# A decoder step on one core: 64 cache copies of 1 MB between the loads, and two samples' keys moved ahead of a weight

## The chip, the cores and the metric

The kernel runs on one core of a Trainium2 chip. The metric is the device time of one execution in microseconds (us). Before the change the median of three runs is 1412.86 us (1412.8 to 1414.62).

## The reference, cut to what matters

One layer is computed for a prompt of 256 tokens and for 8 samples of 4 new tokens each: a mixer with windowed attention, cross-attention to 256 memory tokens, then a mixture of 32 experts. All of it is float32. The parts that the change touches:

```python
k_all = jnp.concatenate([cache_k_win[l], k], axis=1)      # 8 samples, 2048 old rows + 4 new ones, 512 wide
v_all = jnp.concatenate([cache_v_win[l], v], axis=1)
o_a = merge_branches([dilated_branch_sample(q, k_all, v_all, w, d, rel_bias) for (w, d) in DILATED])
...
mk, mv = mem_kv(mem_prompt, g_mem[l], w_xk[l], w_xv[l])   # keys and values of the memory tokens
...
xs = xs + moe(rmsnorm(xs, g_ff[l]), *moe_w)               # 32 experts: w_gate_up 1024x2048, w_down 1024x1024
...
k_win_sample = k_all[:, n_new:]                           # the window moved on by 4 rows: an output
v_win_sample = v_all[:, n_new:]
```

The last two lines make 16 blocks of 2,044 old rows (4.19 MB each, 67 MB in all) that go unchanged from one place in DRAM to another. No engine computes on them: they are plain DMA transfers, here called cache copies. The attention of a sample reads only about 9 rows per partition of its keys and of its values.

## The kernel before, in words

**Work.** The program is written out by hand, engine by engine. It first projects all 288 tokens with `w_in` (TensorE, lines 1436 and 1440), turns and pools, projects the second half of the prompt (line 1520), and then walks over the samples, b = 1 to 7. For each sample VectorE multiplies the window's keys with the four queries (`row`, lines 1129 to 1132, four times a sample), ScalarE takes exponentials, TensorE multiplies with the values (`values`, lines 1628 and 1630). Beside the samples lie `FILL` products: `mk` and `mv`, the memory's keys and values (line 1608), which need `w_xk` and `w_xv`. Then follow the output projection, cross-attention, the router, and a loop over 32 experts (lines 1895 and 1924). The experts' weights go through two buffers, `wide` (gate and up, 8 MB) and `slim` (down, 4 MB), each of which holds one expert; a piece is loaded again as soon as TensorE has read it.

**Buffers of the samples.** `kwin[0]`, `kwin[1]` (the keys of even and odd samples) and `vwin` (values) lie in `wide`, over `w_in`. So a window can be loaded only when the projection has read the pieces of `w_in` below it (`w_read` counts the pieces). A window is four transfers, 1.8 MB together (lines 499 and 502). ScalarE then moves the last rows of a window into place (`late_keys`, `late_values`, line 764) before VectorE or TensorE may use it.

**The order of transfers.** All of this goes out on SyncE's one queue, and the transfers of that queue are served in the order of issue. SyncE waits in its program for what a transfer needs (a free buffer) and then issues it; what stands behind waits too. `copy(n)` issues n cache copies. The list `COPIES` says how many at each of 14 places, and after the first expert's weights `copy(len(pieces))` issues what is left. `slim_round` loads a weight into `slim` (line 495), `window` a sample's keys or values, `step0` the first expert (lines 598 and 602), `step` the others (607 and 610). Before the change a copy is 2 MB, and there are 32 of them: 7 at the first place, 3 between the first expert's two weights, 3 left after them.

Of the kernel before, what the change touches and what calls it, by code (L numbers as in the profile page):

```python
# [8 lines left out]
P = 128  # L9
D = 1024  # L10
KC = D // P
SEQ, DEC_B, DEC_T = 256, 8, 4
# [5 lines left out]
AW = HEADS * HD  # L18
# [80 lines left out]
def build(nc, i, o):  # L99
# [5 lines left out]
    with ctx:  # L105
# [34 lines left out]
        slimf = slim[:, :, :].rearrange("p k n -> p (k n)")  # L140
        kwin = [wf[:, 4608 * s:4608 * s + 4608].rearrange("p (s n) -> p s n", n=AW) for s in range(2)]
        kfirst = slimf[:, 3584:8192].rearrange("p (s n) -> p s n", n=AW)
# [109 lines left out]
        def add(*name):  # L252
            jobs.append(name)
# [14 lines left out]
        for t in range(DEC_T):  # L268
            add("qb", 0, t)
        add("trq", 1), add("trk", 1)  # L270


        COPIES = [7, 1, 1, 1, 1, 2, 1, 2, 2, 2, 3, 2, 1, 3]
        ROUND_AT = {3: 1, 7: 2}
# [11 lines left out]

        add("qb", 1, 0), add("qb", 1, 1)
        for lot in range(2):
# [156 lines left out]
        pieces = []  # L445
        for b in range(DEC_B):
            for src, dst in (("cache_k_win", "k_win_sample"), ("cache_v_win", "v_win_sample")):
                for h in range(2):
                    pieces.append(tuple(ap.rearrange("s h d -> (s h d)").rearrange("(c j a n) -> c a j n", c=2, a=16, j=8)[h]
                                        for ap in (o[dst][0, b, 0:KEEP], i[src][0, b, DEC_T:PAST])))  # L450
# [14 lines left out]
        def _(sp):  # L465
# [4 lines left out]
            load(sp, "gcol", gcol[:, :, :], i["g_all"])  # L470
            load(sp, "rel", rb[0:BUCKETS, :], i["rel_bias"])
            for k in range(KC):
                sp.dma_start(wide[:, k, :], w_in[k]).then_inc(wide_in[k], 16)
            load(sp, "cbias", cb[:, 0:TOEP + 6 * P + 4 * NS], i["c_bias"])
            load(sp, "cfresh", fmask[:, :], i["c_fresh"])
# [4 lines left out]
            load(sp, "iota", iota[:, :], i["c_iota"])  # L480

            def copy(n):
                for _ in range(n):
                    dst, src = pieces.pop(0)
                    sp.dma_start(dst, src).then_inc(stored["copies"], 16)

# [16 lines left out]

            sp.wait_ge(cleared, 1)
            window(kfirst, i["cache_k_win"], 0, k_in[0])
            b, use = place(("tr1", 2, 1))
            sp.wait_ge(bank_full[b], use + 1)
# [8 lines left out]
            copy(COPIES.pop(0))  # L516

            sp.wait_ge(w_read, 5)
            window(kwin[1], i["cache_k_win"], 1, k_in[1])
            sp.wait_ge(w_read, 7)  # L520
# [5 lines left out]
            for b in range(1, DEC_B):  # L526
                if b + 1 < DEC_B:
                    sp.wait_ge(scored, b)
                    window(kwin[(b + 1) % 2], i["cache_k_win"], b + 1, k_in[(b + 1) % 2])
                if b in ROUND_AT:  # L530
                    slim_round(ROUND_AT[b])
                else:
                    copy(COPIES.pop(0))

                bb, use = place(("pv", b - 1))
                sp.wait_ge(bank_full[bb], use + 1)
                window(vwin, i["cache_v_win"], b, v_in)
# [56 lines left out]
            def step0():  # L594

                sp.wait_ge(wide_used, 8)
                for c in range(4):
                    sp.dma_start(wide[:, 2 * c:2 * c + 2, :], gate_up(0, c)).then_inc(wide_in[2 * c], 16)
                copy(COPIES.pop(0))
                for h in range(2):  # L600
                    sp.wait_ge(slim_used, 4 * h + 4)
                    sp.dma_start(slim[:, 4 * h:4 * h + 4, :], down(0, h)).then_inc(slim_in[4 * h], 16)
# [24 lines left out]
            sp.wait_ge(stored["y"], 48)  # L627
            sp.wait_ge(stored["copies"], 16 * 4 * DEC_B)

# [96 lines left out]
        def _(act):  # L726
# [72 lines left out]
            for t in range(2):  # L799
                root(3 + t, P, hn[:, t, :], mkTf[:, 0:D] if t == 0 else mkTf[:, D:2 * D])  # L800
            rows_out(1)
            turned_in(1)
# [42 lines left out]
            unit_exp(0)  # L845
            late_keys(1)
            for lot in range(2):
# [136 lines left out]
        def _(dve):  # L984
# [173 lines left out]
            for b in range(1, DEC_B):  # L1158
                dve.wait_ge(expd, 2 * b)
                share(b - 1, b, P * (UNITS[b - 1][1] + 1))  # L1160
                dve.wait_ge(k_in[b % 2], 64 * (b // 2 + 1))
                dve.wait_ge(late_k, b + 1)
                for t in range(DEC_T):
                    row(b, t)
                    if t < 3:
                        (shift, sums, shares)[t](b - 1)
                    if b >= 2 and t == 0:
                        keep(b - 2)
                    if t == 2:
                        logits(b)  # L1170
                largest_score(b)
# [240 lines left out]
        def _(pe):  # L1412
# [105 lines left out]
            for k in range(KC):  # L1518
# [6 lines left out]
                for t in ROWS_AT.get(k, ()):  # L1525
                    pe.wait_ge(qparts_in, 1)
                    row(0, t)
            turn_rows(1)

# [110 lines left out]

            row(1, 0), row(1, 1)
            for lot in range(2):
# [336 lines left out]
```

## Time and profile before

| what | value |
|---|---|
| median of three runs | 1412.86 us |
| the profiled execution's own time | 1413.55 us |
| its span | 1411.8 us |
| TensorE busy | 1259.9 us (89%) |
| VectorE busy | 482.0 us (34%) |
| ScalarE busy | 234.3 us (17%) |
| DMA, mean over the span | 395 GB/s, 557.14 MB |
| chain that ended last | DMA 50%, PE 38%, DVE 8% |

The span is the stretch between the first and the last instruction of the profiled execution; the execution's own time is 1.75 us more. A busy share is an average over stages that have different limits, so it says little by itself. The rows that are needed stand further down. DMA rows give the time from issue to landing, which contains the time that a transfer waits in the queue.

### The profile page before, as it was taken

To read this page: it belongs to the slowest core of one execution; us is meant where nothing else is said; L and a number is where in the kernel's file an instruction comes from. 1 tells how busy PE (TensorE), PEld (TensorE's weight loads), DVE (VectorE), ACT (ScalarE), POOL (GpSimd) and SP (SyncE) were. 2 spreads that over 40 slices of the span, in tenths; PEclk is the share of its full clock that TensorE was granted. 3 is DMA by queue.
4 is the path that set the end of the run, shared out by engine and by line. 5 is a ranking of instruction groups with operands and counts; after the bars stand their busy time and mean duration, and the time that the engine had idled before them with its cause. 6 is when DMAs were issued, how large, how long until landed. Compare 5 with 4: busy or idle time off the path is not lost.

```text
span 1411.8 us, 16539 instructions
## 1 busy us (share of the span) xinstructions
PE 1259.9 (89%) x6415; PEld 528.3 (37%) x6415; DVE 482.0 (34%) x1019; ACT 234.3 (17%) x460; POOL 68.1 (5%) x69
## 2 busy tenths in 40 slices
PE   6997988988897899999999999999999999999996
PEld 4453333356644433333333333333333333333332
DVE  2267988432326412312132121321213212132124
ACT  1234443211411110110110100111011010011102
POOL 2010000005007000000000000000000000000000
PEclk9998988899997999999999999999999999999998
DMA  9989898998999999999999999999999999999993
GB/s 356 342 307 391 342 394 320 366 385 303 344 365 370 346 417 427 427 428 427 428 429 428 428 430 428 427 430 429 428 428 429 428 428 429 428 428 430 428 427 158
DMA packets 51740, 557.14 MB, mean 395 GB/s; under 512 B 7021, under 2 KB 9301, under 8 KB 15885
## 3 DMA queue, kind: packets, MB, share of 16 engines
q1 hardware_dynamic: 50629, 553.04, 96.0%
q0 software_dynamic: 1072, 3.57, 0.6%
q8 instruction: 26, 0.43, 0.1%
q14 instruction: 13, 0.11, 0.0%
HBM read 552.02 MB, written 71.72 MB: 442 GB/s over the span
## 4 chain that ended last, share of the span: by engine, by line
DMA 50%; PE 38%; DVE 8%; issue 1%; ACT 1%; SPq 1%; DVEq 0%; ACTq 0%
DMA wide<-in_w_gate_up 49%; PE bank L1895 12%; PE bank L1587 3%; PE bank L1608 2%; PE bank L1924 2%; PE bank L1690 2%; PE bank L1630 2%; PE bank L1440 2%; DMA wide<-in_cache_k_win 1%; PE bank L1520 1%; DVE small L1132 1%; PE bank L1436 1%; PE bank L1678 1%; DVE wide L1129 1%; PE bank L1877 1%
## 5 line engine op out<-in xcount | busy, mean ns | idle before, releaser
L1895 PE MATMUL bank<-wide,att 128*64 128x512 f32 x2048 | 463.3, 596 | 58.6 <-DMA wide<-in_w_gate_up 58.4
L1895 PEld LDWEIGHTS bank<-wide,att 128*64 128x64 f32 x2048 | 139.3, 136 | 362.6 <-issue 228.6
L1924 PE MATMUL bank<-slim,att 128*64 128x512 f32 x1024 | 226.8, 595 | 0.0
L1372 DVE TENSOR_SCALAR att<-bank 128x512 f32<-128x512 f32 x32 | 22.1, 692 | 469.1 <-PE bank L1895 469.1
L1924 PEld LDWEIGHTS bank<-slim,att 128*64 128x64 f32 x1024 | 70.6, 137 | 152.2 <-issue 149.2
L1351 DVE TENSOR_TENSOR x<-x,bank 128x512 f32<-128x512 f32 x68 | 46.6, 686 | 233.0 <-PE bank L1877 226.4
L954 ACT ACTIVATE att<-att 128x512 f32<-128x512 f32 x32 | 20.2, 630 | 517.4 <-DVE att L1372 517.4
L1877 PE MATMUL bank<-tb,att 128*128 128x512 f32 (+1 forms) x192 | 84.7, 611 | 1.8 <-issue 1.3
L963 ACT ACTIVATE tb<-bank 64x512 f32<-64x512 f32 x64 | 37.9, 592 | 234.1 <-PE bank L1924 233.7
L1608 PE MATMUL bank<-slim,ta 128*128 128x512 f32 x128 | 59.7, 621 | 3.0 <-DVE wide L1130 3.0
L1132 DVE TENSOR_REDUCE small<-wide 128x24 f32<-128x1536 f32 x28 | 49.1, 1753 | 1.0
L1844 PE MATMUL bank<-att,mkT 128*128 128x128 bf16 x408 | 46.7, 224 | 1.4 <-DVE att L1302 1.4
L1844 PE MATMUL bank<-att,ta 128*128 128x128 bf16 x408 | 46.3, 224 | 0.0
L1630 PE MATMUL bank<-wide,pr 128*32 128x512 f32 x192 | 34.1, 865 | 10.2 <-DVE pr L1111 10.2
L764 ACT ACTIVATE wide<-wide 32x512 f32<-32x512 f32 x60 | 37.6, 626 | 8.9 <-DMA wide<-in_cache_v_win 5.7
L1608 PEld LDWEIGHTS bank<-slim,ta 128*128 128x128 f32 x128 | 24.7, 198 | 36.8 <-issue 36.8
L1129 DVE TENSOR_TENSOR wide<-wide,bank 128x1024 f32<-128x1024 f32 x28 | 33.9, 1212 | 3.1 <-ACT wide L764 3.0
L1690 PE MATMUL bank<-ta,slim 128*128 128x288 f32 x128 | 33.0, 422 | 2.2 <-DVE ta L1020 2.2
L1844 PEld LDWEIGHTS bank<-att,mkT 128*128 128x128 bf16 x408 | 28.7, 100 | 15.2 <-issue 14.6
L1379 DVE TENSOR_TENSOR att<-att 128x512 f32<-128x512 f32 x32 | 33.4, 1045 | 1.1
L959 ACT ACTIVATE att<-bank 128x512 f32<-128x512 f32 x32 | 19.1, 597 | 74.8 <-PE bank L1915 74.8
L1915 PE MATMUL bank<-ident,att 128*128 128x128 f32 x128 | 21.0, 286 | 11.5 <-DVE att L1379 9.6
(279 smaller groups left out, 1153.4 us busy)
## 6 DMA issues: line engine op xcount, KB each, us to landing
wide<-in_w_gate_up SPq DMA_DIRECT2D x128, 2048.0 KB, 25.5
slim<-in_w_down SPq DMA_DIRECT2D x64, 2048.0 KB, 22.0
out_k_win_sample<-in_cache_k_win SPq DMA_DIRECT2D x16, 2044.0 KB, 19.4
out_v_win_sample<-in_cache_v_win SPq DMA_DIRECT2D x16, 2044.0 KB, 27.8
wide<-in_w_in SPq DMA_DIRECT2D x8, 1024.0 KB, 14.2
wide<-in_cache_v_win SPq DMA_DIRECT2D x8, 1024.0 KB, 4.9
wide<-in_cache_mem_k SPq DMA_DIRECT2D x8, 1024.0 KB, 23.5
wide<-in_cache_mem_v SPq DMA_DIRECT2D x8, 1024.0 KB, 13.0
```

The lines of the kernel that those rows point to most:

```text
L963: ins = A(ye[i // 2][CAP * (i % 2):CAP * (i % 2) + CAP, 512 * h:512 * h + 512], bank_y[CAP * h:CAP * h + CAP, :], ACT.Copy)
L1129: V.tensor_tensor(pd[:, 0:2, :], pair, ps[:, :].unsqueeze(1).broadcast_to([P, 2, AW]), ALU.mult)
L1132: link(V.tensor_reduce(S_[b % 2][:, :, t, :], pd.rearrange("p k (h d) -> p k h d", d=HD), AX.X, ALU.add))
L1351: ins = V.tensor_tensor(dst, dst, bk[:, :], ALU.add)
L1587: ins = M(tk[h][0][0:n, :], left[:, k, t0:t0 + n], slim[:, k, 512 * h:512 * h + 512], start=k == 0, stop=k == KC - 1)
L1608: ins = M(ps[:, :], ta[:, k, P * t:P * t + P], slim[:, k, 512 * h:512 * h + 512], start=k == 0, stop=k == KC - 1)
L1630: ins = M(ps[g, :], flat[:, kind, :], vwin[:, 8 if kind == 2 else 4 * kind + t, :], start=k == 0, stop=False)
L1690: ins = M(ps[:, 0:T], slim[:, k, P * c:P * c + P], ta[:, k, :], start=k == 0, stop=k == KC - 1)
L1844: M(bk[:, c:c + 2 * CAP], hparts[t][:, s, P * k:P * k + P], onehot[:, t, :], start=t == 0 and s == 0, stop=False)
L1877: ins = M(out, back[buf][:, t0:t0 + m], ye[buf][:, 512 * h:512 * h + 512], start=True, stop=True)
L1895: ins = M(bk[half[h], :], rows[:, k, :], wide[:, k, c:c + 512], start=False, stop=k == KC - 1)
L1924: ins = M(bank_y[half[h], :], aT[:, f % 4, f // 4, :], slim[:, f, 512 * h:512 * h + 512], start=f == 0, stop=f == KC - 1)
```

## The change

Cache copies are cut in four pieces a block, where there were two: 64 transfers of 1 MB. Their places change. Six go between the eight pieces of `w_in`, two around the keys of sample 0, one ahead of the keys of sample 2, four between the four pieces of the first expert's gate and up weights; `COPIES` (now counted in MB) is set anew, and nine are left behind the first expert. The two key buffers swap places, so that the keys of sample 1 need three pieces of `w_in` read, where they needed five, and those of sample 2 five; both are now issued ahead of `w_xk`. On TensorE the first two query rows of sample 1 come ahead of turning the second half of the prompt; ScalarE moves that sample's late keys earlier; VectorE does its first row ahead of scaling the first unit's shares.

```diff
-        kwin = [wf[:, 4608 * s:4608 * s + 4608].rearrange("p (s n) -> p s n", n=AW) for s in range(2)]
+        kwin = [wf[:, 4608 * s:4608 * s + 4608].rearrange("p (s n) -> p s n", n=AW) for s in (1, 0)]
...
-        add("trq", 1), add("trk", 1)
+        add("qb", 1, 0), add("qb", 1, 1), add("trq", 1), add("trk", 1)
...
-        COPIES = [7, 1, 1, 1, 1, 2, 1, 2, 2, 2, 3, 2, 1, 3]
+        COPIES = [5, 3, 4, 3, 2, 2, 3, 2, 4, 4, 5, 3, 2, 4]
...
-                for h in range(2):
-                    pieces.append(tuple(ap.rearrange("s h d -> (s h d)").rearrange("(c j a n) -> c a j n", c=2, a=16, j=8)[h]
+                for h in range(4):
+                    pieces.append(tuple(ap.rearrange("s h d -> (s h d)").rearrange("(c j a n) -> c a j n", c=4, a=16, j=4)[h]
...
             for k in range(KC):
                 sp.dma_start(wide[:, k, :], w_in[k]).then_inc(wide_in[k], 16)
+                if 0 < k < KC - 1:
+                    copy(1)
...
             sp.wait_ge(cleared, 1)
+            copy(1)
             window(kfirst, i["cache_k_win"], 0, k_in[0])
+            copy(1)
...
+            sp.wait_ge(w_read, 3)
+            window(kwin[1], i["cache_k_win"], 1, k_in[1])
             sp.wait_ge(w_read, 5)
-            window(kwin[1], i["cache_k_win"], 1, k_in[1])
+            copy(1)
+            window(kwin[0], i["cache_k_win"], 2, k_in[0])
             sp.wait_ge(w_read, 7)
             window(vwin, i["cache_v_win"], 0, v_in)
...
             for b in range(1, DEC_B):
-                if b + 1 < DEC_B:
+                if 1 < b < DEC_B - 1:
                     sp.wait_ge(scored, b)
                     window(kwin[(b + 1) % 2], i["cache_k_win"], b + 1, k_in[(b + 1) % 2])
...
                 for c in range(4):
                     sp.dma_start(wide[:, 2 * c:2 * c + 2, :], gate_up(0, c)).then_inc(wide_in[2 * c], 16)
-                copy(COPIES.pop(0))
+                    copy(1)
+                copy(COPIES.pop(0) - 4)
...
             for t in range(2):
                 root(3 + t, P, hn[:, t, :], mkTf[:, 0:D] if t == 0 else mkTf[:, D:2 * D])
+            late_keys(1)
             rows_out(1)
...
             unit_exp(0)
-            late_keys(1)
...
             for b in range(1, DEC_B):
-                dve.wait_ge(expd, 2 * b)
-                share(b - 1, b, P * (UNITS[b - 1][1] + 1))
+                if b > 1:
+                    dve.wait_ge(expd, 2 * b)
+                    share(b - 1, b, P * (UNITS[b - 1][1] + 1))
...
                     row(b, t)
+                    if b == 1 and t == 0:
+                        dve.wait_ge(expd, 2)
+                        share(0, 1, P)
...
+            row(1, 0), row(1, 1)
             turn_rows(1)
...
-            row(1, 0), row(1, 1)
             for lot in range(2):
```

SyncE's queue around `w_xk` (the weight of the memory's keys), before. `in_cache_k_win` into `wide` is a window of keys, `in_cache_v_win` one of values, and a row whose output begins with `out_` is a cache copy:

```order
L499 DMA wide<-in_cache_k_win 128x2048
L502 DMA wide<-in_cache_k_win 32x2048 x3
L499 DMA wide<-in_cache_v_win 128x2048
L502 DMA wide<-in_cache_v_win 32x2048 x3
L495 DMA slim<-in_w_xk 128x1024 x8
L485 DMA out_k_win_sample<-in_cache_k_win 16x8x4088
L499 DMA wide<-in_cache_k_win 128x2048
L502 DMA wide<-in_cache_k_win 32x2048 x3
L485 DMA out_k_win_sample<-in_cache_k_win 16x8x4088
L499 DMA wide<-in_cache_v_win 128x2048
L502 DMA wide<-in_cache_v_win 32x2048 x3
```

The same place after the change:

```order
L501 DMA wide<-in_cache_k_win 128x2048
L504 DMA wide<-in_cache_k_win 32x2048 x3
L475 DMA out_k_win_sample<-in_cache_k_win 16x4x4088
L501 DMA wide<-in_cache_k_win 128x2048
L504 DMA wide<-in_cache_k_win 32x2048 x3
L501 DMA wide<-in_cache_v_win 128x2048
L504 DMA wide<-in_cache_v_win 32x2048 x3
L497 DMA slim<-in_w_xk 128x1024 x8
L475 DMA out_k_win_sample<-in_cache_k_win 16x4x4088 x3
L475 DMA out_v_win_sample<-in_cache_v_win 16x4x4088 x4
L501 DMA wide<-in_cache_v_win 128x2048
L504 DMA wide<-in_cache_v_win 32x2048 x3
```

The keys of sample 2 moved from behind `w_xk` and a copy to ahead of it. Between `w_xk` and the values of sample 1 there stood 4 MB of copies and the keys of sample 2; now there stand 7 MB of copies.

SyncE's queue around the first expert, before (`w_gate_up` and `w_down` are its weights):

```order
L598 DMA wide<-in_w_gate_up 128x4096 x4
L485 DMA out_v_win_sample<-in_cache_v_win 16x8x4088 x2
L485 DMA out_k_win_sample<-in_cache_k_win 16x8x4088
L602 DMA slim<-in_w_down 128x4096 x2
L485 DMA out_k_win_sample<-in_cache_k_win 16x8x4088
L485 DMA out_v_win_sample<-in_cache_v_win 16x8x4088 x2
```

And after the change:

```order
L605 DMA wide<-in_w_gate_up 128x4096
L475 DMA out_k_win_sample<-in_cache_k_win 16x4x4088
L605 DMA wide<-in_w_gate_up 128x4096
L475 DMA out_v_win_sample<-in_cache_v_win 16x4x4088
L605 DMA wide<-in_w_gate_up 128x4096
L475 DMA out_v_win_sample<-in_cache_v_win 16x4x4088
L605 DMA wide<-in_w_gate_up 128x4096
L475 DMA out_v_win_sample<-in_cache_v_win 16x4x4088
L610 DMA slim<-in_w_down 128x4096 x2
L475 DMA out_v_win_sample<-in_cache_v_win 16x4x4088
L475 DMA out_k_win_sample<-in_cache_k_win 16x4x4088 x4
L475 DMA out_v_win_sample<-in_cache_v_win 16x4x4088 x4
```

Six MB of copies stood ahead of `w_down`, now four; six stood behind it, now nine.

## Rows read from the trace of the kernel before

**Rows 1.** The page's 40 slices of the span: busy share of the DMA engines in tenths

```profile
DMA  9989898998999999999999999999999999999993
```

**Rows 2.** The chain that ended last, in order of time: start us, us, what

```profile
50.30 1.94 PE bank L1436 x8
...
106.59 0.74 SPq L495
...
111.22 19.80 DMA wide<-in_cache_k_win
...
1026.17 3.68 PE bank L1895 x16
...
1055.54 3.68 PE bank L1895 x16
```

**Rows 3.** Timeline of SyncE's issues around the first expert: start us, us, line, transfer

```profile
431.11 11.34 SPq L602 DMA_DIRECT2D slim<-in_w_down  x2
...
443.16 1.26 SPq L485 DMA_DIRECT2D out_v_win_sample<-in_cache_v_win  x2
470.46 14.85 SPq L607 DMA_DIRECT2D wide<-in_w_gate_up  x4
```

**Rows 4.** DMA issues, from 442.1, 442.5, 443.8 and 497.0 us: KB each, us to landing

```profile
slim<-in_w_down SPq DMA_DIRECT2D x1, 2048.0 KB, 13.0
out_k_win_sample<-in_cache_k_win SPq DMA_DIRECT2D x1, 2044.0 KB, 18.8
out_v_win_sample<-in_cache_v_win SPq DMA_DIRECT2D x1, 2044.0 KB, 29.5
...
slim<-in_w_down SPq DMA_DIRECT2D x1, 2048.0 KB, 9.3
```

**Rows 5.** Timeline of SyncE's issues of sample 1's two windows

```profile
93.67 0.35 SPq L499 DMA_DIRECT2D wide<-in_cache_k_win  x1
...
130.40 0.33 SPq L499 DMA_DIRECT2D wide<-in_cache_v_win  x1
```

**Rows 6.** DMA issues, from 93.7, 106.6, 111.9, 134.3 and 135.0 us: us to landing

```profile
wide<-in_cache_k_win SPq DMA_DIRECT2D x1, 1024.0 KB, 4.7
...
slim<-in_w_xk SPq DMA_DIRECT2D x1, 512.0 KB, 14.2
...
out_k_win_sample<-in_cache_k_win SPq DMA_DIRECT2D x1, 2044.0 KB, 24.6
...
wide<-in_cache_k_win SPq DMA_DIRECT2D x1, 256.0 KB, 12.1
...
out_v_win_sample<-in_cache_v_win SPq DMA_DIRECT2D x1, 2044.0 KB, 16.4
```

**Rows 7.** DMA issues, the first and the seventh of seven copies, from 29.1 and 33.1

```profile
out_k_win_sample<-in_cache_k_win SPq DMA_DIRECT2D x1, 2044.0 KB, 17.3
...
out_v_win_sample<-in_cache_v_win SPq DMA_DIRECT2D x1, 2044.0 KB, 51.7
```

**Rows 8.** Timelines of DVE and ACT: idle time before a row in brackets, then its releaser

```profile
108.88 1.22 DVE L1129 TENSOR_TENSOR wide<-wide,bank 128x1024 f32<-128x1024 f32 x1 [2.00 <-ACT wide L764]
...
133.67 1.22 DVE L1129 TENSOR_TENSOR wide<-wide,bank 128x1024 f32<-128x1024 f32 x1 [0.97 <-ACT wide L764]
...
149.80 2.54 ACT L764 ACTIVATE wide<-wide 32x512 f32<-32x512 f32 x4
...
153.68 1.21 DVE L1129 TENSOR_TENSOR wide<-wide,bank 128x1024 f32<-128x1024 f32 x1
```

**Rows 9.** Timeline of PE: two pieces of the second projection, and one query row

```profile
85.52 5.31 PE L1520 MATMUL bank<-wide,ta 128*128 128x512 f32 x12
...
93.47 0.38 PE L1514 MATMUL bank<-hn 96*128 96x512 bf16 x1
```

**Rows 10.** DMA issues, the last piece of w_in, from 7.4, and all of w_xv, from 159.2

```profile
wide<-in_w_in SPq DMA_DIRECT2D x1, 1024.0 KB, 21.6
...
slim<-in_w_xv SPq DMA_DIRECT2D x8, 512.0 KB, 8.8
```

More of the change, by code:

```diff
@@ L285, in build @@
             FILL[3 + n, 1].append(("mv", t, h))
-        add("qb", 1, 0), add("qb", 1, 1)
         for lot in range(2):
@@ L471, in _, with copy @@
             load(sp, "rel", rb[0:BUCKETS, :], i["rel_bias"])
+            def copy(n):
+                for _ in range(n):
+                    dst, src = pieces.pop(0)
+                    sp.dma_start(dst, src).then_inc(stored["copies"], 16)
             for k in range(KC):
                 sp.dma_start(wide[:, k, :], w_in[k]).then_inc(wide_in[k], 16)
+                if 0 < k < KC - 1:
+                    copy(1)
             load(sp, "cbias", cb[:, 0:TOEP + 6 * P + 4 * NS], i["c_bias"])
@@ L480, in _ @@
             load(sp, "iota", iota[:, :], i["c_iota"])
[L482 to L485, printed above, removed]
             def slim_round(r):
@@ L627, in _ @@
             sp.wait_ge(stored["y"], 48)
-            sp.wait_ge(stored["copies"], 16 * 4 * DEC_B)
+            sp.wait_ge(stored["copies"], 16 * 8 * DEC_B)
         @block.gpsimd
```

## The prediction

> **What bounds the kernel now.** I read the page's slices first. The DMA engines show 9 tenths or more in every slice but the last from the eleventh on, and a few eights before [rows 1]. Then the chain that ended last: in the second half it repeats one pattern, a wait for the next expert's weights and 3.68 us of products, every 1055.54 - 1026.17 = 29.37 us [rows 2]. An expert is six loads of 2 MB, so a load costs 29.37 / 6 = 4.9 us, and from the second expert on the DMA queue alone sets the pace. So the end moves exactly as far as the moment at which expert 1's six loads are through. That is the last load's landing, 497.0 + 9.3 = 506.3 us [rows 4].
>
> What sets 506.3? The queue is served in order. Ahead of expert 1 stand `w_down`'s second half and then 6 MB of copies. The half is issued at 442.1, when TensorE has read the buffer (the second of two issues that end at 442.45 [rows 3]), and lands 13.0 later, at 455.1; the last copy lands at 443.8 + 29.5 = 473.3 [rows 3, 4]. TensorE frees the first piece for expert 1 at 470.46 [rows 3]. So two things end there within 3 us of each other: the copies and the compute ahead of them. Moving copies earlier alone wins little; **the compute before 442 must get shorter, or nothing does.**
>
> **What a copy costs.** Seven copies of 2 MB issued in a row land from 29.1 + 17.3 = 46.4 to 33.1 + 51.7 = 84.8 [rows 7]: 6.4 us each, 3.2 per MB. Three behind `w_down` take 473.3 - 455.1 = 18.2, or 3.03 per MB. A lone one, behind which the queue is empty, lands at 135.0 + 16.4 = 151.4, 5.0 after the window ahead of it (134.3 + 12.1 = 146.4) [rows 6]: 2.5 per MB. A 1 MB copy between loads was never run. Its bounds are 2.5 and 3.2; in a run of several I take 3.1, nearest to the rows of runs, singly 2.5 to 3.2. The Trainium skill (HBM Reference, Specifications) gives a memory domain about 716 GB/s. A copy reads and writes, so by it a copy can go no faster than half of that, an estimate of 2.9 us per MB. The runs of copies agree nearly, the lone one is faster; by 2.9 the sum below would be +1.0 in place of +3.3.
>
> **The change part by part.**
>
> *Six copies between the pieces of `w_in`.* The last piece landed at 7.4 + 21.6 = 29.0 [rows 10]. Six copies add 15 to 19 us: 44 to 48. TensorE starts on that piece at 50.30 [rows 2]. Cost nothing; the cover is TensorE's own pace, and 2 us of it remain at worst. The same copies left the first place, so by about 88 us as many MB are through as before.
>
> *Keys of samples 1 and 2.* The chain shows 19.80 us on keys that stood behind `w_xk` [rows 2]. This is the tempting row. But VectorE's own rows say that sample 2's first row waited only 0.97 us for them [rows 8]: the rest of the 19.8 lay beside TensorE's `mk` products. So this part is worth 0.97, and for sample 1 the 2.00 in the same view. Two query rows put ahead of the turning cost TensorE 2 x 0.38 [rows 9]. In all between -3 and +0.8 at sample 2; but what follows decides, because it is a later wait for the same engine.
>
> *What is late next: the keys of sample 3.* They are issued behind the values of sample 1, and both now stand behind 7 MB of copies that follow `w_xk`.
> - Before: the first window was issued at 93.67, `w_xk` was through at 106.59 + 14.2 = 120.8 [rows 2, 5, 6], 27.1 later.
> - Now the first window waits for three pieces. Two pieces run from 85.52 for 5.31 [rows 9], so the third is read at 88.2. Then 88.2 + 27.1 = 115.3, plus what was put in between: one copy (2.5 to 3.2) and one window. Sample 1's values and sample 3's keys landed 146.4 - (111.9 + 24.6) = 9.9 after the copy ahead of them [rows 6], so a window is 5.0. `w_xk` is through at 123.1.
> - Seven copies at 3.1 are 21.7: 144.8. The values, whose buffer was free at 130.4 [rows 5], and the keys: 9.9 more, 154.7.
> - ScalarE's 2.54 [rows 8] and 0.1: VectorE may start sample 3 at 157.3. It started at 153.68 [rows 8]. **Late by 3.6.**
>
> Behind VectorE's row wait the scores, TensorE's values of sample 2 and the fills. From there to 442 the view of waits has none of VectorE or TensorE on a DMA that could take it back, so 3.6 is carried. The ends: at 2.5 per copy the keys are in time, and 0.97 is won; at 3.2, and with the copies before 88.2 not through by then (84.8, then a bias table of 1 MB at 2.5 and a 2 MB copy at 4.9 to 6.4, about 93 against 88.2 + 2.2), late by 4.7 + 3 = 7.7.
>
> *The first expert.* `w_down`'s second half is issued at 442.1 + 3.6 = 445.7. Only 4 MB of copies stand ahead of it, so its queue is empty by then. From an empty queue 1 MB landed in 4.7 [rows 6], 2 MB then in 7.2: 452.9, where it was 455.1. Nine copies at 3.03 are 27.3: 480.2. Six loads, 29.4: 509.6, against 506.3. TensorE's releases (470.46 + 3.6) come before that and cost nothing. So here the end stands at the delay less 0.3.
>
> **Sum.** +3.3 us on the span of 1411.8. The profiled execution took 1413.55, 0.05% over the median of 1412.86; on the median this is 1416.2. Ends of this case: +8.9 with 7.7 late and nine copies at 3.2 (442.1 + 7.7 + 7.2 + 28.8 + 29.4 = 515.2), about 1421.8; at the other end no delay.
>
> **The rivals.**
>
> 1. *Short copies run like a lone one*, at 2.5 per MB, because loads or the shorter piece let the writes follow. Then sample 3's keys are in time and the nine copies take 22.5: 442.1 + 7.2 + 22.5 + 29.4 = 501.2. But expert 1's last load is issued by TensorE's release at 497.0 and takes 7.2 from an empty queue: 504.2 at the earliest. So -2.1 to 0: 1410.8 to 1412.9, mostly no change. For it: the lone copy. Against it: every run of copies.
> 2. *The front gets shorter, the end is faster.* Both waits of [rows 8], 2.00 and 0.97, are won and reach 442, and the copies go at 2.5. Then 497.0 - 3.0 + 7.2 = 501.2, which is -5.1: 1407.8. It decides from the seven copies' end: before 153.68 - 2.6 - 9.9 = 141.2 sample 3 doesn't wait, before 138.2 all of the 3.0 is won. At 2.5 a copy I get 140.3, so `w_xk` must also be through 2 us sooner than I add up. Against it: the two waits lie beside `mk`, which needs `w_xk`, and by my sum that comes 2 us later than it did.
> 3. *A transfer has a fixed part that 32 more transfers pay.* From an empty queue a 1 MB window took 4.7, of which 2.5 is transfer; 32 times 2.2 are 70: about 1483. Against it: eight transfers of 512 KB had a median of 8.8 to landing [rows 10]; at 2.2 more for each, the fourth and fifth would need some 13. The Trainium skill (DMA: Bandwidth & Descriptors, Bandwidth and Anatomy of one DMA) fits 2.0 us a transfer plus the bytes, and advises 1 MiB or more; by that this would cost 64 us. The row speaks against its holding in a full queue.
> 4. *The first projection waits for `w_in`.* If a piece slows by 0.8 beside its copy, at 3.2 a copy, the last lands at 29.0 + 6 x 4.0 = 53, 2.7 too late, on top of the delay: 1419.
>
> **How the numbers follow.** The forecast has 0.50, rival 1 0.27, rival 2 0.13, rival 3 0.03, rival 4 0.07. A difference under 0.2%, 2.8 us, can't be told from none here. Of the forecast's case some two thirds lie above that (0.33), with rivals 3 and 4 0.43 slower. Rival 2 and a bit of 1 are 0.16 faster. The rest, 0.41, is no change. The forecast's own range is 1412.5 to 1421.8. The range given leaves out rivals 2 (most of it) and 3 and the forecast's far end: 1410.5 to 1420.5.
>
> **What would show it.** In the profile after: a copy of the seven behind `w_xk` taking about 3.1; sample 1's values and sample 3's keys landing near 150 and 155; ScalarE waiting for a window's DMA at line 764's place, then VectorE, at 142 to 157; the last copy ahead of expert 1 near 480; 29.37 unchanged. If the keys of sample 3 land before 151 the forecast's main term is wrong; if `w_down`'s second half is issued before 442, the front got shorter and rival 2 has it; if TensorE waits for `w_in`, rival 4.

## The result, and the profile after

The changed kernel took 1417.89 us (median of 9 runs, 1415.62 to 1420.88) against 1411.94 for the kernel before (9 runs, 1409.44 to 1414.62). The ratio is 1.0041, 95% interval 1.0032 to 1.0051: slower by 0.41%. The profiled execution took 1416.6 with a span of 1414.7, 2.9 more than before's 1411.8. Executions of either kernel differ by some 5 us among themselves, and the two profiles show about half of the 5.95 us that the medians show; that will matter.

The page's DMA slices differ from [rows 1] in one place, a 7 for an 8 in the seventh slice, 212 to 248 us:

```profile
DMA  9989897998989999999999999999999999999993
```

The chain that ended last, of the changed kernel, in order of time (start us, us, what):

```profile
50.02 1.94 PE bank L1448 x8
...
104.86 18.35 DMA slim<-in_w_xk
...
131.89 17.88 DMA wide<-in_cache_v_win
...
153.10 4.91 PE bank L1643 x24
...
1029.13 3.68 PE bank L1907 x16
1058.50 3.68 PE bank L1907 x16
```

Three things answer to [rows 2]. TensorE is on the last piece of `w_in` at 50.02, where it was at 50.30. An expert still takes 1058.50 - 1029.13 = 29.37. And the wait of 19.80 for the keys of sample 2 is gone from the chain, but a wait of 17.88 has come in its place, for the **values of sample 1**. (Ahead of it stand 18.35 for `w_xk`; TensorE itself waited only 0.16 us for that weight.)

SyncE's issues around the first expert (timeline, to be read against [rows 3]):

```profile
433.13 9.73 SPq L610 DMA_DIRECT2D slim<-in_w_down  x2
...
470.75 14.84 SPq L615 DMA_DIRECT2D wide<-in_w_gate_up  x4
493.81 3.77 SPq L618 DMA_DIRECT2D slim<-in_w_down  x2
```

DMA issues (KB each, us from issue to landing): the last piece of `w_in`, from 12.3; the last of `w_xk`, from 104.9; the last of the seven copies behind it, from 112.9; the end of sample 3's keys, from 134.3; `w_down`'s second half, from 442.5; the last of the nine copies left, from 448.4; expert 1's last load, from 497.2:

```profile
wide<-in_w_in SPq DMA_DIRECT2D x1, 1024.0 KB, 33.8
...
slim<-in_w_xk SPq DMA_DIRECT2D x1, 512.0 KB, 18.4
...
out_v_win_sample<-in_cache_v_win SPq DMA_DIRECT2D x1, 1022.0 KB, 32.5
...
wide<-in_cache_k_win SPq DMA_DIRECT2D x1, 256.0 KB, 19.8
...
slim<-in_w_down SPq DMA_DIRECT2D x1, 2048.0 KB, 7.8
...
out_v_win_sample<-in_cache_v_win SPq DMA_DIRECT2D x1, 1022.0 KB, 31.0
...
slim<-in_w_down SPq DMA_DIRECT2D x1, 2048.0 KB, 12.7
```

Add the two columns: `w_in` is through at 46.1, `w_xk` at 123.2, the seven copies at 145.4, sample 3's keys at 154.1, `w_down` at 450.3, the nine copies at 479.4, expert 1's last load at 509.9. In the kernel before that last load landed at 506.3 [rows 4]: **+3.6, and the span grew by 2.9.**

Where did it go wrong in the front? TensorE's values of sample 1 (24 products), before:

```profile
148.35 2.78 PE L1630 MATMUL bank<-wide,pr 128*32 128x512 f32 x24
```

and in the changed kernel, with ScalarE's rows that stand ahead of them and VectorE's first row of sample 3:

```profile
149.79 2.54 ACT L772 ACTIVATE wide<-wide 32x512 f32<-32x512 f32 x4 [10.44 <-DMA wide<-in_cache_v_win]
152.36 0.60 ACT L839 ACTIVATE hn<-bank 128x512 f32<-128x512 f32 x1
...
153.10 4.91 PE L1643 MATMUL bank<-wide,pr 128*32 128x512 f32 x24 [5.55 <-ACT hn L839]
...
156.75 1.22 DVE L1137 TENSOR_TENSOR wide<-wide,bank 128x1024 f32<-128x1024 f32 x1 [2.06 <-ACT wide L772]
```

ScalarE works in order. It stands 10.44 us at sample 1's late values, whose window is behind seven copies; the emptying of a bank (L839) is queued behind that, and TensorE waits 5.55 us for the bank. Its products start 4.75 late and take 4.91 for 2.78. TensorE's windows of 148 to 153 and 153 to 158 us tell why (stretch, us, busy, granted clock, DMA share, GB/s):

```profile
148.00:153.00 5.00, 0.00 (x0) 0.76 1.05 442
153.00:158.00 5.00, 4.90 (x28) 0.56 0.53 226
```

It did nothing in the first, and in the second most of the time was granted at 1.2 GHz of the two levels, 1.2 and 2.4.

VectorE starts sample 3 at 156.75, 3.07 late [rows 8]. But its lateness doubles when it next needs TensorE's results, which reach it through ScalarE. The same row of VectorE, before and in the changed kernel:

```profile
162.11 0.38 DVE L1106 TENSOR_REDUCE small<-pr 128x32 f32<-128x128 f32 x1
...
168.18 0.38 DVE L1114 TENSOR_REDUCE small<-pr 128x32 f32<-128x128 f32 x1 [3.02 <-ACT pr L847]
```

It is 6.07 late there, and 3.02 of that is this wait. So TensorE's lateness at the values, and not VectorE's own at the keys, is the larger one from here on.

### The profile page after: what moved, and what is told of

Same layout as the page of the kernel before. It is cut to its first block, busy times and chain, and to the rows that moved or that the text cites. A ratio compares the mean times of both kernels' runs of the same rounds, so it can differ in the third digit from the quotient of the medians.

```text
span 1414.7 us, 16571 instructions
## 1 busy us (share of the span) xinstructions
PE 1259.5 (89%) x6415; PEld 528.6 (37%) x6415; DVE 476.9 (34%) x1019; ACT 234.2 (17%) x460; POOL 68.3 (5%) x69
## 4 chain that ended last, share of the span: by engine, by line
DMA 51%; PE 37%; DVE 8%; issue 1%; ACT 1%; SPq 1%; DVEq 0%; ACTq 0%
DMA wide<-in_w_gate_up 49%; PE bank L1907 12%; PE bank L1600 3%; PE bank L1936 2%; PE bank L1702 2%; PE bank L1621 2%; PE bank L1643 2%; PE bank L1452 2%; DMA slim<-in_w_xk 1%; PE bank L1532 1%; DMA wide<-in_cache_v_win 1%; PE bank L1448 1%; DVE small L1140 1%; PE bank L1690 1%; DVE wide L1137 1%
## 5 line engine op out<-in xcount | busy, mean ns | idle before, releaser
L962 ACT ACTIVATE att<-att 128x512 f32<-128x512 f32 x32 | 20.2, 630 | 520.1 <-DVE att L1384 520.1
## 6 DMA issues: line engine op xcount, KB each, us to landing
wide<-in_cache_mem_k SPq DMA_DIRECT2D x8, 1024.0 KB, 22.2
```

## The experiments

Every run is given as a ratio to runs of the kernel before that were taken beside it, with its 95% interval. Two theories stood after the first reading. **A**: the nine copies left behind `w_down` make the end, and the front's lateness is given back, since `w_down`'s second half is issued at 442.54 and was at 442.12. **B**: sample 3's lateness is carried to the end, as predicted.

**1. The new order of the keys alone.** The changed kernel with the copies of the kernel before:

```diff
-        COPIES = [5, 3, 4, 3, 2, 2, 3, 2, 4, 4, 5, 3, 2, 4]
+        COPIES = [7, 1, 1, 1, 1, 2, 1, 2, 2, 2, 3, 2, 1, 3]
```
(with the 2 MB pieces, and without the copies put singly between loads)

> The changed kernel with its copies put back as they were before (32 transfers of 2 MB, none between the pieces of w_in, two transfers behind w_xk, 6 MB left behind the second half of expert 0's w_down); what stays of the change is the order of the keys: samples 1 and 2 ahead of w_xk, sample 1's first two rows and its late keys earlier. Theory A (the copies left at the end made the loss, the keys are worth next to nothing because the front gives back what it gains or loses): within 1.5 us of the kernel before, h1 issued between 441.5 and 443 us, expert 1's last load at 505.5 to 507.5 us. Theory B (what sample 3 loses or gains is carried to the end): w_xk now stands behind 1.5 MB more, so v(1) and sample 3's keys land about 3 us later than before; 2 to 3 us slower than before.

Measured: 1.0008 (0.9994 to 1.0021). That can't be told from none, and it leaves room for up to 3 us, as theory B had it. In the profiled execution `w_down`'s second half was issued at 444.58 and expert 1's last load landed at 510.1, so both of theory A's ranges (441.5 to 443, and 505.5 to 507.5) were missed.

**2. The size alone.** The kernel before, each copy cut in two in its place (`COPIES` is doubled with it):

```diff
-                for h in range(2):
+                for h in range(4):
```

> The kernel before with nothing changed but the size: each 2 MB transfer becomes two of 1 MB in the same place (64 transfers, 6 MB left behind w_down). Theory A: the queue is full behind these transfers, so a cut costs nothing that the clock can tell: within 0.2% of before, the six left taking 18 to 19.5 us together. Rival 1 of the prediction (short transfers run nearer to the pace of a lone one): up to 2 us faster. Rival 3 (a fixed part for each transfer, 32 more of them): many times 10 us slower.

Measured: 0.9996 (0.9986 to 1.0006). Thirty-two more transfers cost nothing; six 1 MB copies took 18.2 us as three of 2 MB had. So the new size makes none of the loss, and the new order of the keys at most about half of it. What is left is where the copies stand.

**3 and 4. Three copies fewer behind `w_xk`, or three fewer at the end.** Both put three into places where the queue ran dry (first the list with fewer behind `w_xk`, then the one with fewer left):

```diff
-        COPIES = [5, 3, 4, 3, 2, 2, 3, 2, 4, 4, 5, 3, 2, 4]
+        COPIES = [5, 3, 1, 3, 2, 3, 3, 4, 4, 4, 5, 3, 2, 4]
...
+        COPIES = [5, 3, 4, 3, 2, 3, 3, 4, 4, 4, 5, 3, 2, 4]
```

> The changed kernel with 4 MB instead of 7 MB behind w_xk; the three go to places where its queue ran dry (one more behind sample 5's keys, two more behind sample 7's), so 9 MB are left at the end as in the changed kernel. Sample 3 should start on VectorE at its old time or before (153 to 154 us instead of 156.75). Theory B (the lateness is carried): 3 us faster than the changed kernel, so about 1.002 of before. Theory A (the front gives it back by 442 us, the nine left make the end): h1 issued within 1 us of the changed kernel's 442.5 us, expert 1's last load at 509 to 510.5 us, no more than 1 us faster than the changed kernel, 1.003 to 1.005 of before.

> The changed kernel with 7 MB behind w_xk as it has them, and the three extra copies in the same dry places as in the run beside it taken from the nine left at the end: 6 MB are left, as in the kernel before. Theory A: the six take 18 to 19.5 us behind h1's landing at 450 to 451 us, expert 1's last load lands at 500 to 502 us instead of 509.9 unless the release by TensorE holds it (then about 503 to 505): 5 to 9 us faster than the changed kernel, 0.998 to 1.001 of before. Theory B (sample 3's lateness sets the end, 3 us of it): no more than 3 us faster than the changed kernel beyond what the lateness gives, 1.002 or more of before.

Measured: 1.0007 (0.9994 to 1.0020) with fewer behind `w_xk`, 1.0028 (1.0016 to 1.0040) with fewer left. **A has the order wrong**: three fewer in front recover most of the changed kernel's 1.0041 (B's 1.002 lies at the end of the interval). Three fewer at the end recover 0.0013, which the intervals can't tell from nothing. From the run with fewer behind `w_xk`, TensorE's values and SyncE's issue of expert 1's first piece (timeline):

```profile
146.62 2.78 PE L1643 MATMUL bank<-wide,pr 128*32 128x512 f32 x24
...
466.92 14.84 SPq L615 DMA_DIRECT2D wide<-in_w_gate_up  x4
```

and the last copy, from 444.6, and expert 1's last load, from 493.4 (DMA issues):

```profile
out_v_win_sample<-in_cache_v_win SPq DMA_DIRECT2D x1, 1022.0 KB, 34.1
...
slim<-in_w_down SPq DMA_DIRECT2D x1, 2048.0 KB, 14.6
```

The values start at 146.62 with no wait and at full pace, and TensorE frees expert 1's first piece at 466.92, where the changed kernel did at 470.75: 3.83 earlier, so **the lateness is carried**. But the nine copies are through only at 444.6 + 34.1 = 478.7, and hold the last load at 508.0. From the run with fewer left, the same of SyncE's timeline:

```profile
472.44 14.85 SPq L615 DMA_DIRECT2D wide<-in_w_gate_up  x4
```

and the same two DMA issues, from 449.3 and 498.9:

```profile
out_v_win_sample<-in_cache_v_win SPq DMA_DIRECT2D x1, 1022.0 KB, 24.6
...
slim<-in_w_down SPq DMA_DIRECT2D x1, 2048.0 KB, 9.2
```

Here the copies are through at 449.3 + 24.6 = 473.9, but TensorE frees the piece only at 472.44, and the last load (issued at 498.9) lands at 508.1. Each run shows the bound that the other one took away.

That is **theory C**: the end is the later of two things. One is TensorE's release of expert 1's first piece plus 35.7 us (506.3 - 470.46 = 35.8 in the kernel before, 508.1 - 472.44 = 35.7 here). The other is the last copy's landing plus six loads, 29.3 (508.0 - 478.7 with fewer behind `w_xk`). The two figures are read from these three profiles, so it is the others that test it.

**5 to 8. Both at once; `w_in`; twelve left; the kernel before with four left.**

Cut to what matters, in this order; the first three against the changed kernel, the last against the kernel of run 2:

```diff
-        COPIES = [5, 3, 4, 3, 2, 2, 3, 2, 4, 4, 5, 3, 2, 4]
+        COPIES = [5, 3, 1, 3, 3, 3, 3, 4, 4, 4, 5, 3, 3, 5]
...
+        COPIES = [11, 3, 4, 3, 2, 2, 3, 2, 4, 4, 5, 3, 2, 4]
...
-                if 0 < k < KC - 1:
-                    copy(1)
...
+        COPIES = [5, 3, 1, 3, 2, 2, 3, 2, 4, 4, 5, 3, 2, 4]
...
-        COPIES = [14, 2, 2, 2, 2, 4, 2, 4, 4, 4, 6, 4, 2, 6]
+        COPIES = [14, 2, 2, 2, 3, 4, 3, 4, 4, 4, 6, 4, 2, 6]
```

> The changed kernel with 4 MB behind w_xk (three fewer) and 6 MB left at the end (three fewer); the six go one each to places where the queue ran dry: behind samples 3's, 5's keys and the router weight's copies, two behind sample 7's keys, one before w_down (five there instead of four). Theory C, formed from the first four runs (the end is the later of two: TensorE's release of expert 1's first piece plus 35.7 us, as in the kernel before, or the last left copy's landing plus 29.3 us; sample 3's lateness does reach the release): release at 467 us, copies through at 468 to 471, expert 1's last load at 502 to 504.5 us, about 1409 to 1411 us, 0.997 to 0.9995 of before, and 3 to 5 us faster than the run with 4 MB behind w_xk and nine left. Theory B alone (only the lateness counts): as the run with nine left, 1.0007 of before. Theory A alone (only the copies left count): as the run with 7 MB and six left, 1.0028.

> The changed kernel with the six copies between the pieces of w_in moved behind the memory prompt's load, so that w_in lands as before; all else as in the changed kernel (7 MB behind w_xk, nine left). Theory C: the copies between w_in's pieces are hidden, so the same as the changed kernel within 1 us: 1.003 to 1.005 of before. Rival 4 of the prediction (the first projection waits for w_in): 2 to 3 us faster than the changed kernel, 1.002 or less.

> The changed kernel with 4 MB instead of 7 MB behind w_xk and the three put at the end, so 12 MB are left. Theory C: release as in the run with 4 MB and nine left (467 us), but twelve copies at 3.2 to 3.6 us run to 488 to 490 us, expert 1's last load at 517 to 519 us: 9 to 11 us slower than the run with nine left, 1.0065 to 1.0085 of before. Theory B alone (the lateness of sample 3 counts, the copies left do not): as the run with nine left, 1.0007.

> The kernel before with its copies cut to 1 MB in the same places (0.9996 of before in the first four runs) and two of the six left at the end moved up: one behind sample 3's keys, one behind sample 6's, where its queue was dry for 3.6 and 3.8 us. The order of the keys stays as before. Theory C: the copies are through by 468 to 469 us, so only the release holds, at 468 to 471 us: expert 1's last load at 503.5 to 506.5 us, 0 to 2.5 us faster than with six left, 0.998 to 0.9995 of before. Theory A alone: 6 us faster, 0.9955 of before. No gain at all would say that the release held that kernel already.

Measured: both at once 0.9996 (0.9981 to 1.0011), `w_in` alone 1.0062 (1.0042 to 1.0082), twelve left 1.0091 (1.0072 to 1.0110), four left 0.9999 (0.9986 to 1.0012). With both at once, the release in SyncE's timeline:

```profile
464.95 14.85 SPq L615 DMA_DIRECT2D wide<-in_w_gate_up  x4
```

and the last copy and the last load, from 440.3 and 491.5 (DMA issues):

```profile
out_v_win_sample<-in_cache_v_win SPq DMA_DIRECT2D x1, 1022.0 KB, 24.6
...
slim<-in_w_down SPq DMA_DIRECT2D x1, 2048.0 KB, 9.2
```

With twelve left, the same timeline:

```profile
470.33 14.84 SPq L615 DMA_DIRECT2D wide<-in_w_gate_up  x4
```

and the same DMA issues, from 449.9 and 496.8:

```profile
out_v_win_sample<-in_cache_v_win SPq DMA_DIRECT2D x1, 1022.0 KB, 39.7
...
slim<-in_w_down SPq DMA_DIRECT2D x1, 2048.0 KB, 23.6
```

In the first the copies are through as the first load is issued, and 464.9 + 29.3 = 494.2 would be their bound; the release holds, 464.95 + 35.7 = 500.7, and the load lands at 500.6. In the second the copies hold: 489.6 + 29.3 = 518.9, and it lands at 520.5. All four ratios lie above what theory C expected (0.9995, 1.005, 1.0085 and 0.9995 at most); all four intervals reach into their ranges. Four left gained nothing on six: the kernel before was held by the release already, and this theory A had as 6 us. With both at once the whole loss is gone, with the new size and the new order of the keys still in, so the loss is made by where the copies stand. But a gain on the kernel before, as theory C had it, isn't shown: the interval holds B's 1.0007 as well, and it is twelve left (1.0091, where B had 1.0007) that tells C from B by time. Theory C over the first ten profiles (us; R the release, C the last copy's landing):

| kernel | R | C | later of R + 35.7, C + 29.3 | last load landed | ratio |
|---|---|---|---|---|---|
| before | 470.5 | 473.3 | 506.2 (R) | 506.3 | 1 |
| changed: 7 MB behind `w_xk`, 9 left | 470.8 | 479.4 | 508.7 (C) | 509.9 | 1.0041 |
| 4 MB, 9 left | 466.9 | 478.7 | 508.0 (C) | 508.0 | 1.0007 |
| 7 MB, 6 left | 472.4 | 473.9 | 508.1 (R) | 508.2 | 1.0028 |
| 4 MB, 6 left | 465.0 | 464.9 | 500.7 (R) | 500.6 | 0.9996 |
| 4 MB, 12 left | 470.3 | 489.6 | 518.9 (C) | 520.5 | 1.0091 |
| before, 1 MB copies, 4 left | 466.5 | 463.5 | 502.2 (R) | 502.2 | 0.9999 |
| keys alone | 473.1 | 475.8 | 508.8 (R) | 510.1 | 1.0008 |
| 1 MB copies alone | 467.9 | 474.4 | 503.7 (C) | 506.0 | 0.9996 |
| copies out of `w_in` | 480.1 | 489.6 | 518.9 (C) | 520.1 | 1.0062 |

It holds within 2.3 us everywhere; where it is 1 to 2 short, one or more of the loads took about 6 us in place of 4.9. And in all fourteen profiles, those of runs 9 to 12 too, the span ends 904.5 to 906.0 us after that landing, so the landing sets the time of an execution, as the prediction had it.

One caution: a landing is read from a single execution, a ratio from many. Both at once took 1408.4 in its profile with a median of 1411.2, copies out of `w_in` 1426.7 with 1422.4, and keys alone 1416.6 with 1414.8. So the table tests the rule, and what a placement is worth stands in the ratios.

In two profiles the release itself is late and needs a reason: 480.13 in the `w_in` run, and 470.33 in the run with twelve left, 3.4 later than in the run with nine, from nearly the same front.

**9 to 12. A chance meeting of VectorE and GpSimd.** The profiles differ most between the issue of `w_xq` and that of sample 6's `cache_mem_k`: 348.76 - 293.16 = 55.6 us in the kernel before, 347.49 - 297.80 = 49.7 in the changed one. It is this 5.9 that made the front's lateness, still 4.64 at `w_xq`, vanish in the profiled pair. There VectorE moves eight small blocks of the xq projection (128 by 32) while GpSimd subtracts the experts' bias rows. Before, the timeline of GpSimd, VectorE and TensorE:

```profile
336.11 8.19 POOL L682 TENSOR_TENSOR att<-att 32x2048 f32<-32x2048 f32 x2 [8.23 <-issue]
...
340.88 3.45 DVE L1218 COPY att<-tb 128x32 f32<-128x32 f32 x1 [0.68 <-ACT tb L888]
...
344.39 1.07 PE L1701 MATMUL bank<-att 128*32 128x256 f32 x16 [3.98 <-DVE att L1218]
```

and TensorE's window behind it (stretch, us, busy, granted clock, DMA share, GB/s):

```profile
345.00:350.00 5.00, 5.00 (x45) 0.66 0.44 137
```

In the changed kernel, the same timeline:

```profile
340.35 8.22 POOL L690 TENSOR_TENSOR att<-att 32x2048 f32<-32x2048 f32 x2 [8.45 <-issue]
...
343.87 0.57 DVE L1230 COPY att<-tb 128x32 f32<-128x32 f32 x1 [3.70 <-ACT tb L896]
...
344.49 1.07 PE L1713 MATMUL bank<-att 128*32 128x256 f32 x16 [1.10 <-DVE att L1230]
```

and the same window:

```profile
345.00:350.00 5.00, 5.00 (x51) 1.00 0.49 167
```

The block takes 0.18 us where GpSimd doesn't meet it. Here it ends with the subtraction that it falls into: at 344.33, with the pair (336.11 + 8.19 = 344.30), or at 344.44, with the first of two of 4.1 each (340.35 + 4.11 = 344.46). TensorE waits 3.98 or 1.10. After 3.98 its granted clock averages 0.66 over the next 5 us, so most of them ran at 1.2 GHz instead of 2.4; after 1.10 it stays at 1.00. Behind the last block nothing hides it. Of the 5.9 us, some 2.9 are this wait and 1.4 the stretch behind it. The other 1.7 fall earlier, before GpSimd's work begins: TensorE needs 6.29 us from its first product of xq to VectorE's first copy in the kernel before, at a granted clock of 0.73 after a wait of 2.25, and 4.60 in the changed one, at 1.00 after 0.69.

The runs with nine and with twelve left (both 4 MB behind `w_xk`) show the meeting best: they issue `w_xq` at 292.03 and 291.99, the block takes 0.77 and 2.22 us, and sample 6's `cache_mem_k` is issued at 343.71 and 347.56. In the `w_in` run the block took 3.84. The Trainium skill (SBUF — State Buffer, Who interferes with whom) says that VectorE, in its modes that use two ports, and GpSimd contend for a shared pair of ports, and that whoever issues second stands still for the whole instruction of the other; the trace agrees for this copy, to 0.03 us at the ends.

Four runs moved the bias rows' loads ahead of four loads of `cache_mem_v`, to bring GpSimd's work before the last block (that the meeting hid the lateness is theory D):

```diff
+            for s in range(3):
+                load(sp, f"braw{s}", braw[32 * s:32 * s + 32, :], i["b_gate_up"][0])
             for b in range(4):
                 cache_mem(cmem[4 + b], "cache_mem_v", b, cv_in[b])
-            for s in range(3):
-                load(sp, f"braw{s}", braw[32 * s:32 * s + 32, :], i["b_gate_up"][0])
```

> The changed kernel with the three loads of the experts' bias rows put ahead of the four cache_mem_v loads of the first half instead of behind them; nothing else. In the ten traces so far GpSimd's two subtractions on these rows (4.1 us each) start 0.3 to 4.8 us before VectorE's last small copy of the xq projection; the copy takes 0.2 us alone and up to 3.8 us, to the end of the subtraction that it falls into, and TensorE waits for it. Theory D (this chance meeting is what gave the changed kernel's lateness back in the profiled pair: 3.45 us in the kernel before, 0.57 in the changed one): with the rows landing some 8 to 10 us earlier the last copy takes 0.2 to 0.5 us, the release of expert 1's first piece comes at 469 to 471 us, and as the nine copies left still hold the end, the gain is small: 1.002 to 1.004 of before, 0 to 3 us faster than the changed kernel. Rival: the time does not move with it, 1.004 to 1.005.

> The kernel before with the same one move of the bias rows' loads; its copies as they were (32 of 2 MB, 6 MB left). Theory D: the last xq copy takes 0.2 to 0.5 us instead of 3.45, TensorE's clock does not fall behind it, cache_mem_k of sample 6 is issued at 342 to 346 us instead of 348.76, the release comes at 465 to 468 us, and the end is then held by the six copies (through at 470 to 473 us, plus 29.3) or the release plus 35.7: expert 1's last load at 501 to 504 us, 0.9970 to 0.9990 of before. Rival (the meeting has nothing to do with the end): 0.9995 to 1.0005.

> The run with 4 MB behind w_xk and six left (0.9996 of before) with the same one move of the bias rows' loads. Theories C and D: nothing but the release holds this kernel, so what the move gives comes through whole: the last xq copy 0.2 to 0.5 us instead of 1.35, less spread between executions, release at 462 to 465 us, expert 1's last load at 498 to 501 us, 0.9960 to 0.9985 of before. Rival: 0.9990 to 1.0005, as without the move.

> The run with the copies between w_in's pieces moved behind the memory prompt (1.0062 of before, with the last xq copy at 3.84 us in its profile) and the same one move of the bias rows' loads. Theory: that run was not slow by w_in but by this meeting; without it, it equals the changed kernel with the same move within 1.5 us, 1.002 to 1.0045 of before. Rival (copies between w_in's pieces are worth 2 to 3 us, so taking them out costs that): 1.004 to 1.0065, 2 us or more above the run beside it.

Measured: the changed kernel with the move 1.0076 (1.0063 to 1.0089), before 1.0007 (0.9995 to 1.0019), six left 0.9990 (0.9976 to 1.0005), copies out of `w_in` 1.0083 (1.0068 to 1.0098). **The move misses its aim**, and none of the four ratios lies in the range that theory D gave it; the third is its rival's. The changed kernel with the move:

```profile
343.79 4.05 POOL L694 TENSOR_TENSOR att<-att 32x2048 f32<-32x2048 f32 x1
...
345.51 2.37 DVE L1230 COPY att<-tb 128x32 f32<-128x32 f32 x1 [3.70 <-ACT tb L896]
...
347.94 1.07 PE L1713 MATMUL bank<-att 128*32 128x256 f32 x16 [2.91 <-DVE att L1230]
```

GpSimd has a third subtraction 4 us after the pair, and the move has brought that one onto the last block (in the third run it is the cast behind it). The block took 2.37, 2.45, 1.74 and 0.67 us in the four. So that the meeting moves the front in one execution is shown, by its rows; that it shifts the median of a kernel is not. What these runs do show: with and without copies between `w_in`'s pieces, side by side on one chip, 1421.7 and 1421.8 us. A cost of those copies isn't seen; with five and six runs one of 2 us could still hide. The interval of the 1.0062 reaches down to 1.0042, so what it has over the 1.005 expected may be chance. Theory C fits these four as well (513.1, 502.7, 506.8 and 512.1 by the rule, 513.1, 505.0, 506.8 and 513.2 landed).

**Open**: the three other kernels with the changed front and nine copies left took 1421.7 to 1422.4, the changed kernel itself 1417.9. It wasn't run beside them, so the chip and the moves can't be told apart. Their nine copies took 29.9 to 32.3 us, the changed kernel's 29.0.

No version beats the kernel before by what a measurement can tell. The best, with 4 MB behind `w_xk`, six left and the bias rows first, took 1410.24 against 1411.73, and the interval of its ratio holds 1.

## Why the prediction was right, and where it was not

- **The outcome was right**: slower was said, and +3.3 at the last load, where +3.6 came. Part of that agreement is luck. The medians moved by 5.95, nearly twice the 3.3, and inside the range: the profiled execution of the kernel before lay 1.6 above its median, that of the changed kernel 1.3 below. And the terms behind the sum were not all right.
- *`w_in`*: right. The last piece landed at 46.1 (44 to 48 was said), TensorE reached it at 50.02 without a wait. Rival 4 falls.
- *Keys of samples 1 and 2 worth almost nothing*: right. Their rows start 3.1 and 1.5 us earlier (105.78 and 132.13), and the order alone gives 1.0008, with no gain to be seen. The 19.80 of the chain was indeed the tempting row.
- *`w_xk`, seven copies, sample 3*: right in size. 123.2 (123.1 said), 22.2 for seven (21.7), keys at 154.1 (154.7), VectorE 3.07 late (3.6).
- *Which engine*: wrong. The text followed sample 3's keys to VectorE. The values of sample 1, issued ahead of them, do more: behind ScalarE's in-order wait they hold a bank, and TensorE is late by 4.75 at the values and by 6.9 at the `mk` products behind them (158.93 where it was 152.06). VectorE, 3.07 late by the keys, is 6.07 late once it has waited for TensorE. I had the values' landing, but took no account of who waits for them. What each of the two alone would cost wasn't run: both stand behind the same copies.
- *"so 3.6 is carried"*: in the profiled pair it is not, 442.54 against 442.12; against the run that differs only in three copies it is, 442.54 against 438.72, and the release 3.83. The step was sound; the pair hid it, in the main since the kernel before lost 3.45 us to GpSimd in its profiled execution and the changed one 0.57. I had read "no wait that could take it back" from one execution, and had not asked which of its waits were chance.
- *The first expert*: `w_down` 7.8 from issue to landing (7.2 said), the nine copies 29.0 (27.3 said: 3.2 per MB, not 3.03), six loads 30.5 (29.4). Together 3.5 over the sum, and the issue 3.2 under it: the total was right because these two cancelled, which is luck. TensorE's releases "cost nothing" was nearly false too: with the 9.2 that the last load takes behind its other half, in place of 7.2, the release gives 497.0 + 3.6 + 9.2 = 509.8, as late as the copies' 509.6.
- *"either the compute before 442 or nothing"*: half. The kernel before was held by TensorE's release alone (506.2 against 502.6 by the copies), so fewer copies left gain nothing in it, as said. But nine left put the copies' bound above, and three more put another 10 us on it.
- Rival 1 falls: in runs of six to twelve, copies of 1 MB took 3.0 to 3.6 us each. Single ones did run like the lone one: the pieces of `w_in` and the copies between them landed mostly some 2.5 apart, copy after piece, so the 2.9 estimated as the fastest is no floor. (With 2.9 for each of the two runs of copies the sum comes to +0.7, not to the +1.0 that was written.) Rival 2: the front got longer. Rival 3: 32 more transfers cost nothing, 0.9996; the row of eight small loads was the better guide.

## What to carry to other kernels

When two chains meet at one point, write down both bounds as a later-of-two and test each with the other out of the way; a change that relieves one shows nothing while the other holds. A window that you move ahead lets something else stand at the back of the queue: follow each operand behind the new run of transfers to every engine that waits in order behind its consumer, not only to the next use of the thing you moved. And a wait read from a single execution may be chance; a second profile of a near twin shows which waits stay.

## What the runs showed that I had not expected

- VectorE's 128 by 32 copy, 0.18 us alone, took up to 4.02 when it fell into a GpSimd subtraction of 32 by 2048, and ended with it. Behind the one of 3.45 TensorE waited 3.98 us, and its clock fell to an average of 0.66. The length of the wait alone doesn't decide that: after 2.91 and 2.98 in two runs it stayed at 1.00, after 2.27 in a third it averaged 0.66.
- Copies left behind the first expert cost more each where there are more: four took 2.9 us each, six 3.0 to 3.2, nine 3.2 to 3.6, twelve 3.3. What sets this wasn't tried.
- The release counts for 35.7 us, of which the last load is 9.2 from an empty queue, not the 7.2 that I had added up: its two halves are issued 3.4 apart and follow one another.
